# Decode states as whole channel-major buffers, decode tile normalised first, last output tiles among the first FFN pairs

## The reference

```python
h = rmsnorm(x, g_pre_mix) * (1 + sc1) + sh1
v_pool, x_conv, gate_b, gate_c = split(h @ w_in)
pool_in = concat([pool_buf, v_pool])          # pool_buf: 15 rows
y_pool = pool_mixer(pool_in, pos0, pool_w, pool_scale)   # windows 2/4/8/16
conv_in = concat([conv_buf, gate_c * x_conv]) # conv_buf: 2 rows
y_conv = gate_b * causal_dwconv(conv_in, conv_w)
mix = concat([y_pool, y_conv]) @ w_out
x = x + gt1 * rmsnorm(mix, g_post_mix)
h2 = rmsnorm(x, g_pre_ffn) * (1 + sc2) + sh2
ffn_in = concat([ffn_buf, h2 @ ffn_w_up])     # ffn_buf: 2 rows
a, b = split(causal_dwconv(ffn_in, ffn_conv_w))
x = x + gt2 * rmsnorm((silu(a) * b) @ ffn_w_down, g_post_ffn)
return x, pool_in[:, -15:], conv_in[:, -2:], ffn_in[:, -2:]
```

## Time and profile before

| | us |
|---|---|
| median of 3 runs | 797.73 (797.41 to 799.37) |
| profiled execution, its own time | 796.71 |
| span of its slowest core (core 6) | 795.2 |
| PE busy | 717.5 (90%) |
| DVE busy | 488.9 (61%) |
| ACT busy | 337.4 (42%) |
| POOL busy | 206.1 (26%) |

### The profile page before, as it was taken

How to read it: one execution, slowest core, us unless ns; L and a number is a source line. 1 busy time by engine, 2 the same in 40 slices (tenths; PEclk the granted TensorE clock), 3 DMA queues, 4 the chain that set the end, 5 groups by cost and what they waited for, 6 DMA issues and landing times.

```text
span 795.2 us, 12501 instructions; the slowest of 8 cores (788.0 to 795.2 us)
## 1 busy us (share of the span) xinstructions
PE 717.5 (90%) x4204; PEld 351.4 (44%) x4204; DVE 488.9 (61%) x660; ACT 337.4 (42%) x607; POOL 206.1 (26%) x266
## 2 busy tenths in 40 slices
PE   0269498998999999999999999999999999999995
PEld 0224254444444554444444444444444444444442
DVE  1246278686687787777767732227888888832222
ACT  1226235644565466655444421114544445422221
POOL 4001010011010001543444420003667667530000
PEclk9979599999899999999999999999999999999999
DMA  8999977319942496488874523234344343003321
GB/s 152 200 191 218 200 186 187 106 54 193 214 150 93 115 239 201 80 166 155 152 141 80 79 54 131 104 110 108 56 83 75 63 85 67 1 13 139 116 78 40
DMA packets 27211, 96.88 MB, mean 122 GB/s; under 512 B 4741, under 2 KB 4997, under 8 KB 26236
## 3 DMA queue, kind: packets, MB, share of 16 engines
q0 software_dynamic: 11904, 47.85, 35.7%
q1 hardware_dynamic: 15244, 48.23, 18.3%
HBM read 125.61 MB, written 18.66 MB: 181 GB/s over the span
## 4 chain that ended last, share of the span: by engine, by line
PE 80%; DMA 11%; DVE 3%; ACT 3%; issue 2%; POOL 1%; DVEq 0%; another core or an unknown queue 0%; ACTq 0%; POOLq 0%; SPq 0%
PE ps L785 50%; PE ps L290 20%; PE ps L281 6%; DMA arena<-w_in_p 5%; DMA arena<-x 3%; DMA arena<-w_ada 2%; PE ps L298 2%; PE ps L736 1%; ACT arena L687 1%; DVE arena L935 1%; ACT arena L540 1%; POOL arena L521 1%; DVE arena L1220 0%; DVE arena L1224 0%; DVE arena L939 0%
## 5 line engine op out<-in xcount | busy, mean ns | idle before, releaser
L785 PE MATMUL ps<-arena 128*128 128x512 bf16 (+1 forms) x2400 | 442.6, 346 | 12.4 <-DMA arena<-w_in_p 6.1
L785 PEld LDWEIGHTS ps<-arena 128*128 128x128 bf16 x2400 | 201.9, 99 | 242.1 <-issue 24.5
L290 PE MATMUL ps<-arena 128*128 128x512 bf16 (+1 forms) x748 | 162.9, 379 | 0.0
L1220 DVE SCALAR_TENSOR_TENSOR arena<-ps,arena 128x1023 f32<-128x1023 f32 x88 | 112.7, 1281 | 53.8 <-ACT arena L1218 53.5
L1234 POOL TENSOR_TENSOR arena<-arena 128x1024 bf16<-128x1024 f32 x44 | 103.6, 2354 | 86.7 <-DVE arena L1224 61.5
L1224 DVE SCALAR_TENSOR_TENSOR arena<-ps,arena 128x1022 f32<-128x1022 f32 x88 | 112.8, 1281 | 9.2
L290 PEld LDWEIGHTS ps<-arena 128*128 128x128 bf16 (+1 forms) x748 | 73.6, 99 | 86.7 <-issue 0.4
L540 ACT ACTIVATE arena<-ps 128x1024 f32<-128x1024 f32 (+1 forms) x34 | 34.8, 1023 | 155.6 <-PE ps L290 128.5
L547 DVE RECIPROCAL arena<-arena 128x1 f32<-128x1 f32 (+1 forms) x68 | 10.8, 158 | 143.8 <-ACT arena L542 143.7
L1218 ACT ACTIVATE arena<-ps,arena 128x1024 f32<-128x1024 f32 x88 | 97.5, 1109 | 0.1
L1217 ACT ACTIVATE arena<-ps 128x2 f32<-128x2 f32 x88 | 15.1, 172 | 129.8 <-PE ps L785 117.3
(11 more groups left out here) (89 smaller groups left out, 381.8 us busy)
## 6 DMA issues: line engine op xcount, KB each, us to landing
arena<-w_up POOLq DMA_DIRECT2D x44, 512.0 KB, 6.2
arena<-x SPq DMA_DIRECT2D x32, 512.0 KB, 8.0
y<-arena SPq DMA_DIRECT2D x32, 512.0 KB, 2.7
arena<-w_ada POOLq DMA_DIRECT2D x24, 512.0 KB, 16.1
arena<-y SPq DMA_DIRECT2D x16, 512.0 KB, 3.7
arena<-w_down POOLq DMA_DIRECT2D x3, 1536.0 KB, 15.2
arena<-w_in_j POOLq DMA_DIRECT2D x4, 768.0 KB, 54.6
arena<-rows SPq DMA_DIRECT2D x4, 512.0 KB, 15.8
```

Of the source, the lines that this page charges most:

```text
L290: inst = e.matmul(out_ap, lhs_list[i], rhs_list[i], start=(first and i == 0), stop=(last and i == n - 1))
L785: inst = e.matmul(o_, l_, r_, start=st, stop=sp_)
L1220: K.op("dve", lambda e: e.scalar_tensor_tensor(tv[:, 1:1024], psv[:, 0:1023], fw_of(1, c), tv[:, 1:1024], ALU.mult, ALU.add), reads=rp + [ ...
```

## The change

States are laid out by the host with channels on partitions and are moved as whole buffers, in and out, so that all 108 transposes of states go, with their evictions and the small buffers SMPP, SMP2 and STG. The state buffers go out with the rows that were carried in still in them, and the host cuts. The two-token tails of the prompt FFN stand in a buffer of their own (STFP). The decode tile is normalised with tiles 0 to 3 and transposed before the first item. `state_in` waits for P0.0 and is written ahead of tiles 6 and 7, `rows1_in` behind item 2. Output tiles 13, 14 and 15 stand behind FFN pairs 0, 1 and 2, on the next bank pair, and what hung on them moves down four to seven pairs. The planner gets another rate for the DMA engines and a second track for SP's queue.

```diff
-DMA_US_PER_BYTE = 1.0 / 380e3
+DMA_US_PER_BYTE = 1.0 / 340e3
...
-                bus = max(bus, free[e] + 1.5) + o.nbytes * DMA_US_PER_BYTE
-                o.fin = bus + 0.5
+                move = o.nbytes * DMA_US_PER_BYTE
+                if e == "pool":
+                    bus = max(bus, free[e] + 1.5) + move
+                    o.fin = bus + 0.5
+                else:
+                    side = max(side, free[e] + 1.5) + 1.7 * move
+                    bus += move
+                    o.fin = side + 0.5
...
     for t in range(4):
         h_act(t)
         h_dve(t)
+    h_load(16)
+    h_act(16)
+    h_dve(16)
...
     def state_in(deps):
-        dma1("sp", STG0[0:120, :], stp_d[0:120, :], writes=[r_stg[0]], deps=deps)
-        dma1("sp", STG1[0:120, :], stp_d[120:240, :], writes=[r_stg[1]], deps=deps)
-        dma1("sp", STG2[0:32, :], stc_d, writes=[r_stg[2]], deps=deps)
...
+        dma1("sp", VS.rearrange("p a b c -> p (a b c)"), stp_d, writes=r_vs, deps=deps)
+        dma1("sp", QS.rearrange("p a b c -> p (a b c)"), stc_d, writes=r_qs, deps=deps)
...
+    samp_tr_ev(2, XN2[0], r_xn2[0], G1T, S1T, [r_g1, r_s1], HS, 0, r_hs)
...
-            if n == 2:
-                h_load(16, deps=[firsts[1]])
-                h_act(16)
-                h_dve(16)
...
-            if c == 0:
-                samp_tr_ev(misc_bank(), XN2[0], r_xn2[0], G1T, S1T, [r_g1, r_s1], HS, 0, r_hs)
...
         if n == 1:
-            rows1_in([firsts[1]])
-            state_in([firsts[1]])
+            state_in([firsts[0]])
+        if n == 2:
+            rows1_in([firsts[2]])
...
     def state_out():
...
+        out_ops.append(dma1("sp", nps_d, VS.rearrange("p a b c -> p (a b c)"), reads=r_vs, deps=[last_pw]))
+        out_ops.append(dma1("sp", ncs_d, QS.rearrange("p a b c -> p (a b c)"), reads=r_qs, deps=[last_pw]))
+        out_ops.append(dma1("sp", npc_d, flat(NPC), reads=r_npc))
...
     o_tile(16, 2)
+    b2(10)
     o_tile(11, 0)
...
-    o_tile(13, 0)
-    b2(12)
...
-    o_tile(14, 2)
-    b2(13)
...
-    o_tile(15, 0)
-    b2(14)
...
     def hook0(i):
-        if i == 0:
+        if i < 3:
+            o_tile(13 + i, next_pair())
+            b2(12 + i)
+        if i == 3:
             b2(15)
-        if i in (1, 2, 3, 4):
-            h2_T(3, i - 1, 6 + i % 2, "act")
-        if i == 4:
+        if i in (4, 5, 6, 7):
+            h2_T(3, i - 4, 6 + i % 2, "act")
+        if i == 7:
             p1y()
-        if i in (5, 8, 11, 14):
-            load_wdn((i - 5) // 3)
-        if 6 <= i < 18 and i % 2 == 0:
-            ffn_state_piece((i - 6) // 2, 6 + (i // 2) % 2)
+            dma1("sp", flat(STF), stf_d, writes=[r_stf])
+        if i in (8, 10, 12, 14):
+            load_wdn((i - 8) // 2)
...
+    out_ops.append(dma1("sp", nfs_d, flat(STF), reads=[r_stf]))
+    out_ops.append(dma1("sp", nfp_d, flat(STFP), reads=r_stfp))
```

More of the change, by code:

```diff
@@ L312, in build_program @@
     cT_d = din("cT", [D, 18])
-    stp_d = din("st_pool", [NS * PB, 512])
-    stc_d = din("st_conv", [NS * 2, 512])
-    stf_d = din("st_ffn", [NS * 2, 2 * DFF])
+    stp_d = din("st_pool", [128, 4 * NS * (PB + DS)])
+    stc_d = din("st_conv", [128, 4 * NS * (2 + DS)])
+    stf_d = din("st_ffn", [128, NCH * 32])
     wada_d = din("w_ada", [24 * 128, KC * 256])
@@ L327, in build_program @@
     y_d = dout("y", [NTOK, D])
[L328 to L333, removed]
+    npc_d = dout("npc", [128, 4 * (PB + 2)])
+    nfp_d = dout("nfp", [128, NCH * 2])
+    nps_d = dout("nps", [128, 4 * NS * (PB + DS)])
+    ncs_d = dout("ncs", [128, 4 * NS * (2 + DS)])
+    nfs_d = dout("nfs", [128, NCH * 32])
     ARENA_BYTES = 207 * 1024
@@ L378, in build_program @@
     TMP = alloc([128, D], F32)
+    IDF = TMP[:, 0:128]
     h2a_off = cur[0]
@@ L833, in P_item @@
         else:
-            K.op("pool", lambda e: e.tensor_copy(SMPP[:, g, TS:TS + PB], V[:, 513:528]), reads=[rV], writes=[r_smpt[g]])
+            K.op("pool", lambda e: e.tensor_copy(NPC[:, g, 0:PB], V[:, 513:528]), reads=[rV], writes=[r_npc[g]])
         if samp:
@@ L838, in P_item @@
             ps3 = PS[:, sbank, 0:TS]
[L840 to L843, removed]
+            K.op("act", lambda e: e.activation(out=v3[:, :, PB:PB + DS], in_=ps3.rearrange("p (s r) -> p s r", r=DS),
+                                               func=AF.Copy), reads=[r_ps[sbank]], writes=[r_vs[g]])
             srcb, rsrc = vf, r_vs[g]
@@ L904, in V_item @@
         else:
-            K.op("pool", lambda e: e.tensor_copy(SMP2[:, j, 32:34], Q[:, 512:514]), reads=[rQ], writes=[r_smp2t[j]])
+            K.op("pool", lambda e: e.tensor_copy(NPC[:, j, PB:PB + 2], Q[:, 512:514]), reads=[rQ], writes=[r_npc[4 + j]])
         if samp:
@@ L1147, in load_wdn @@
         dma1("pool", flat(WDN[:, i0:i1, :]), wdn_d[:, i0 * D:i1 * D], writes=[r_wdnq[q]], sem=s_wdnq[q])
-    STA = TMP
-    r_sta = r_tmp
-    s_sta = new_sem("sta")
-    def ffn_state_piece(n, bank):
-        q0, q1 = n * 8, min(NCH, n * 8 + 8)
-        nq = q1 - q0
-        dma1("sp", STA[0:32, 0:nq * 128], stf_d[:, q0 * 128:q1 * 128], writes=[r_sta], sem=s_sta)
-        K.op("pe", tr_group([PS[:, bank, q * 32:(q + 1) * 32] for q in range(nq)],
-                            [STA[0:32, q * 128:(q + 1) * 128] for q in range(nq)], IDF[0:32, 0:32]),
-             reads=[r_sta, r_id], writes=[r_ps[bank]])
-        K.op("act", lambda e: e.activation(
-            out=STF[:, q0:q1, 0:32], in_=PS[:, bank, 0:nq * 32].rearrange("p (q r) -> p q r", q=nq),
-            func=AF.Copy), reads=[r_ps[bank]], writes=[r_stf])
     def fw_of(kk, c):
@@ L1363, in build_program @@
             down_b(t - 1)
-            for _ in range(2):
-                if so:
-                    ffn_state_out(so.pop(0))
     return finish()
@@ L1389, with cmaj, rmaj @@
     w_up_ = np.ascontiguousarray(f(ffn_w_up)[0][:, perm])
-    state_ffn = np.ascontiguousarray(state_ffn[:, :, perm])
+    state_ffn = state_ffn[:, :, perm]
+    def cmaj(a, pad):
+        s_, r_, f_ = a.shape
+        a = a.reshape(s_, r_, f_ // 128, 128).transpose(3, 2, 0, 1)
+        a = np.concatenate([a, np.zeros(a.shape[:3] + (pad,), np.float32)], axis=3) if pad else a
+        return np.ascontiguousarray(a.reshape(128, -1))
+    def rmaj(a):
+        return np.ascontiguousarray(a.reshape(a.shape[0], a.shape[1], -1).transpose(2, 1, 0).reshape(-1, a.shape[1] * 128))
     vecs = np.concatenate([
@@ L1414 @@
         m["cT"] = np.ascontiguousarray(np.concatenate([c_prompt[i:i + 1], c_sample[sl], np.zeros((1, D), np.float32)], axis=0).T)
-        m["st_pool"] = np.ascontiguousarray(state_pool[sl].reshape(NS * PB, 512))
-        m["st_conv"] = np.ascontiguousarray(state_conv[sl].reshape(NS * 2, 512))
-        m["st_ffn"] = np.ascontiguousarray(state_ffn[sl].reshape(NS * 2, 2 * DFF))
+        m["st_pool"] = cmaj(state_pool[sl], DS)
+        m["st_conv"] = cmaj(state_conv[sl], DS)
+        m["st_ffn"] = cmaj(state_ffn[sl], 0)
         in_maps.append(m)
```

109 lines of the change are left out of this document (28 added, 81 removed).

## The result

| | us |
|---|---|
| before, median | 797.57 (797.19 to 799.37) |
| changed kernel, median | 808.2 |
| ratio, changed to before | 1.012, interval 1.0093 to 1.0147 |
| profiled execution, own time (span of core 4) | 808.18 (806.6) |

The change costs some 9.6 us (7.4 to 11.7). 790 was forecast, 782 to 798. (One execution of each of several kernels ran with a whole die at a lower clock; medians include it, ratios don't, so I compare ratios and turn them into us at 797.6.)

The account below looks back on a forecast made before the run. PE was taken as the bound from 323 to 787 us, with a hole before that from waits for DMA. The terms gave 796.7 - 9.2 - 0.5 + 2.0 = 789.0, or 790.0 on the median's scale; range 782 to 798.

Parts of the forecast that it names:

- Part 1: State transposes in PE's chain go, with nothing hiding them; the whole-buffer DMAs in their place cost nothing: 9.2 us gain.
- Parts 2 and 3: Decode tile with the first tiles, and new order on ACT and SP: together 0.5 us gain.
- The count by rows: Time of the two state transfers ahead of tiles 6 and 7, priced by rows: 11.6 us, the figure taken.
- the count by bytes: The same two state transfers priced by bytes: 9.7 us, so tiles 6 and 7 land 1.9 us earlier.
- The hole: PE's waits before the first decode-column item (P1.0), 15 us with lost clock; nearly all given back, net 0.1 us gain.
- I put the new loss at 1.3 more: O0 and O1 now nearly adjacent on one bank pair, so PE waits for ACT and DVE: 1.3 us more loss.
- the gain of 1.7 at P1.0: P1.0 and V1.0 run in 8.0 us, not 9.7, as no hole lowers the clock shortly before them.
- Rival (b): Before P1.0, ACT's late squares hold PE's banks and cost more than the st_pool wait: 796 us; chance 0.18.
- the two signs of being wrong: Tile 7's square starting before 78 or after 88 us, or PE losing over 6 us between 270 and 330.
- Part 4: Output tiles 13 to 15 among FFN pairs: eight more ACT table loads, 2.0 us loss, bounds -1 to +8.
- rival (c): Eight table loads on the FFN path cost 10.3 us, parts 2 and 3 turn to -4: 803 us; chance 0.10.
- Rival (a): Before P1.0 the hole is really returned: tiles 6, 7 earlier, clock kept in shorter holes; some 784 us; chance 0.22.

Follow-up runs that it names:

- e4_states: The kernel before with only the states as whole channel-major buffers, front, tail and planner as before; ratio 0.9879, 9.7 us faster than before.
- e7_pin: The changed kernel with the squares of tiles 4 to 11 held on ACT behind the copies they stood behind before; ratio 1.0022.
- e13_norms: e7_pin with the DVE norms of tiles 12 and 13 also held ahead of the window sums of P1.2 and P1.3; ratio 0.9864.
- e1_planner: The changed kernel with only the planner's DMA model put back as before (one track for all queues); ratio 0.9972, 795.4 us.
- e9_pin2: e7_pin with the squares of tiles 14 and 15 also held, behind the small pool product's copies of the decode columns; ratio 1.0038.
- e16_pins_tail: e13_norms with output tiles 13 to 15 back ahead of the FFN, as before; ratio 0.9821, 14.3 us under before.
- e2_tail: The changed kernel with output tiles 13 to 15 and what hung on them back ahead of the FFN; ratio 1.0066, 802.9 us.
- e6_states_tail: e4_states with output tiles 13 to 15 behind FFN pairs 0 to 2, planner and front of before; ratio 0.9954.
- e17_norms_only: The changed kernel with only the norms of tiles 12 and 13 held ahead of the window sums, squares left in place; ratio 1.0072.

## Why the prediction was wrong

**Part 1, 9.2 us: right.** e4_states gives 9.7 (8.3 to 11.0).

**Parts 2 and 3 up to P1.0: right to 0.2 us on this core.** P0.1 started at 56.9 (58.2 forecast), the squares of tiles 6 and 7 at 78.05 and 83.00 (78.8 and 83.5 landings), P1.0 at 101.3 (101.1). From tile 5's square (61.44, also waiting for its load) to tile 6's it is 16.6 us. The count by rows gives 16.3 for that and the count by bytes 14.4 (14.2, since the 818 KB are 800 in the unit in which a tile is 512), so the rows fit better. The hole is given back as forecast, and e7_pin shows what that cost: with the squares of tiles 4 to 11 behind the copies P1.0 starts 8.1 us earlier. P1.0 and V1.0 took 8.2 us (6.04 and 2.13), as forecast.

**The step that failed is the end of Part 3, "I put the new loss at 1.3 more".** From P1.0 to the FFN the account has +14.2 us where this step and the gain of 1.7 at P1.0 gave -0.4. I had read the order only where a hole was already known and took the rest as unchanged with one small loss. But the planner's second track moved squares and norms everywhere. The norms of tiles 12 and 13 went from 147 and 154 us to 171 and 188, so that tile 15's load slid into w_ada's burst (PE: 10.7 at 210.8); and tile 11's square waited 8.9 us ahead of the copy of V1.0's decode columns (PE: 5.7 at 123). Undoing the planner's model alone gives 11.8 us, more than the 9.6 by which the change is slower, and its trace gives 14.5 us back in this very stretch. Of the places, the norms are shown: 12.6 us on top of e7_pin. Tile 11's is not, as no run took that wait away. With ten instructions held (e13_norms) the changed planner's order is 8.6 us faster than the old one's (e1_planner), so the new order is not bad as a whole. Rival (b) had PE waiting behind ACT's squares; for the largest of these waits e9_pin2 shows that the late load made it and not the square's place, and late loads stand in no rival. Neither of the two signs of being wrong appeared: tile 7's square started at 83.0, and PE stood idle for 5.5 us between 270 and 330. What would have told is the time from P1.0 to the end, forecast 3.6 us shorter and in fact 15.3 longer (705.3 against 690.0).

**Part 4, +2.0 us: mis-sized.** It measured 6.7 in the traces, and 3.4 to 6.0 between kernels that differ in the tail (e16_pins_tail, e2_tail, e6_states_tail). The count of eight more table loads was right, 13 against 5 before:

```profile
L546 ACT ACT_TABLE_LOAD x7 | 9.0, 1283 | 0.5
L1228 ACT ACT_TABLE_LOAD x6 | 7.7, 1283 | 3.8 <-DVE arena L1167 3.7
```

On core 4 the loss is PE's waits of 2.8 and 2.1 us and the lower clock behind each, 1.7 us: 8.3 in all, where before PE lost 2.4. No load leads to the first wait. Two lead to the second, and whether it would go with them is not measured. So rival (c) is neither shown nor excluded as a part of the cost; in full it is excluded, since its eight loads on the path are 10.3 us and PE's two waits are 4.9, of which 2.8 have nothing to do with loads. The rest of its 803 us, parts 2 and 3 turning from +0.5 to -4, fell far short: they measured -14.3. The Trainium skill (ScalarE: Activation LUTs, What ACT_TABLE_LOAD costs) gives a load and a drain for each switch, by its figures an estimate of 21 us of ACT's time for eight. The rows don't show the drain: the load at 350.41 starts 0.01 us behind the silu, and the root starts 0.02 us behind the load.

**Rival (a)'s premise fell:** that a hole shorter than 9.3 us leaves the clock alone. On core 4 the wait of 2.8 us until 315.3 was followed by the lower clock. (On four of the eight cores the same wait was followed by matmuls at full clock.)

**Open:** why the squares and the norms together give 20.4 us (1.0120 to 0.9864) where alone they give 7.8 and 3.8. One part shows in the traces: in e17_norms_only the norm of tile 13 still ran as late as 186 us, against 188 in the changed kernel and 173 in e13_norms, so the held order alone did not make it early. And of the tail's 3.4 to 6 us, what the loads and each wait are worth.

## What to carry to other kernels

When a planner's cost model is among the edits, compare the whole order on every in-order engine, not only around the hole that is being mended, and price each place where an instruction that waits for a DMA now stands ahead of one that TensorE needs, or ahead of the one that frees the buffer of a later load. A better total of waiting on one engine tells nothing; an edge that holds one instruction tells what its place is worth, with the others as they stand. Measure parts alone: here a gain of 9.7 us was hidden under losses of other parts. And look in the trace of an experiment for what it was to change: a variable that is read after its loop has ended left one of these as it was, under a name that said otherwise.

## What the runs showed of the hardware

A DVE step (L956) of 0.75 us in the median took 2.94 when it started together with a product on GpSimd of 2.34, and 1.27 when it started behind such a product (timelines of the changed kernel):

```profile
339.59 2.94 DVE L956 TENSOR_SCALAR arena<-arena 128x1024 bf16<-128x1024 f32 x1
339.63 2.34 POOL L1177 TENSOR_TENSOR arena<-arena 128x1024 bf16<-128x1024 f32 x1 [4.02 <-DVE arena L551]
...
350.76 2.33 POOL L1177 TENSOR_TENSOR arena<-arena 128x1024 bf16<-128x1024 f32 x1 [4.85 <-DVE arena L1167]
...
352.38 1.27 DVE L956 TENSOR_SCALAR arena<-arena 128x1024 bf16<-128x1024 f32 x1
```

Both times DVE ended 0.56 us behind the product's end. The lengths agree with the Trainium skill (SBUF — State Buffer, SBUF: two separate sides), by which, for certain DVE steps, the one that starts second is held for the other's whole instruction. By the recorded starts DVE was first the first time, by 0.04 us, and was held all the same.

The same load of 512 KB took 3.4 us to land from 171.9, 19.3 from 188.5, beside four loads of w_ada. PE's waits of 2.8 us until 315.3 and of 2.1 until 353.8 were followed on core 4 by a granted clock of 0.57 over 4 us and 0.79 over 8: 1.7 us lost each time. The same waits don't always do it: behind the 2.8 us, 32 matmuls took 8.75 us on core 6 and 7.07, the time at full clock, on core 1.
